# A decoder step on one core: first unit in four groups of two chunks, wide placeholder products, totals of squares tile by tile

## What is computed

```python
def rmsnorm(x, g):
    y = x * rsqrt(mean(x * x, axis=-1) + EPS)
    return y * g
def swiglu(h, w_in, w_out):
    g, u = split(h @ w_in, 2)          # w_in: 1024 x 5632
    return (silu(g) * u) @ w_out       # w_out: 2816 x 1024
for l in range(2):
    x = x + 0.5 * swiglu(rmsnorm(x, g0), w_in0, w_out0)
    ...                                # mixer
    x = x + 0.5 * swiglu(rmsnorm(x, g2), w_in1, w_out1)
y = rmsnorm(x, g_final)
```

## Time and profile before

| what | value |
|---|---|
| median of 3 runs | 1240.37 us (1240.34 to 1240.64) |
| profiled execution, whole | 1240.44 us |
| its span in the trace | 1238.6 us |
| TensorE busy in the span | 1233.2 us |
| VectorE, ScalarE, GpSimd busy | 726.1, 582.7, 81.1 us |
| DMA | 200.39 MB, mean 162 GB/s |

### The profile page before, as it was taken

How to read it: one execution, slowest core, us unless ns; L and a number is a source line. 1 busy time by engine, 2 the same in 40 slices (tenths; PEclk the granted TensorE clock), 3 DMA queues, 4 the chain that set the end, 5 groups by cost and what they waited for, 6 DMA issues and landing times.

```text
span 1238.6 us, 22056 instructions
## 1 busy us (share of the span) xinstructions
PE 1233.2 (100%) x8875; PEld 1210.4 (98%) x8875; DVE 726.1 (59%) x1127; ACT 582.7 (47%) x936; POOL 81.1 (7%) x99
## 2 busy tenths in 40 slices
PE   9999999999999999999999999999999999999998
PEld 9999999989999999999998999999998999999998
DVE  7656554575777656555564565655467585565443
ACT  6534333464556445443345554534344474544343
POOL 0000000100332000000000000000020110000010
PEclk9999999999999999999999999999999999999999
DMA  8344334543354443334543734334478734433341
GB/s 341 137 161 144 112 132 155 205 147 131 127 164 147 157 166 137 134 121 140 187 166 137 262 136 151 143 105 153 163 277 317 287 139 142 163 135 127 125 156 43
DMA packets 34778, 200.39 MB, mean 162 GB/s; under 512 B 4050, under 2 KB 4186, under 8 KB 19490
## 3 DMA queue, kind: packets, MB, share of 16 engines
q1 hardware_dynamic: 32706, 192.24, 44.0%
q0 software_dynamic: 2016, 7.39, 1.9%
HBM read 193.03 MB, written 6.57 MB: 161 GB/s over the span
## 4 chain that ended last, share of the span: by engine, by line
PE 99%; DMA 0%; SPq 0%; DVE 0%; ACT 0%; issue 0%; DVEq 0%
PE bank L556 30%; PE bank L558 30%; PE bank L557 29%; PE bank L714 1%; PE bank L713 1%; PE bank L712 1%; PE bank L716 1%; PE bank L715 1%; PE bank L1059 1%; DMA xp<-xp_in 0%; PE bank L867 0%; PE bank L822 0%; PE bank L975 0%; PE bank L1001 0%; PE bank L1007 0%; PE bank L955 0%
## 5 line engine op out<-in xcount | busy, mean ns | idle before, releaser
L556 PE MATMUL bank<-h_hi,w_hi 128*128 128x320 f32 x1792 | 555.6, 310 | 0.5 <-DVE h_lo L1682 0.5
L558 PE MATMUL bank<-h_hi,w_lo 128*128 128x320 f32 x1792 | 553.8, 309 | 0.0
L557 PE MATMUL bank<-h_lo,w_hi 128*128 128x320 f32 x1792 | 553.7, 309 | 0.0
L1222 ACT ACTIVATE w_hi<-raw 128x1024 fp32r<-128x1024 f32 (+1 forms) x364 | 331.7, 958 | 440.7 <-PE bank L558 421.7
L1668 DVE TENSOR_TENSOR w_lo<-raw,w_hi 128x1024 fp32r<-128x1024 f32 (+1 forms) x364 | 388.5, 1108 | 133.1 <-ACT w_hi L1222 133.0
L556 PEld LDWEIGHTS bank<-h_hi,w_hi 128*128 128x128 f32 x1792 | 336.3, 188 | 2.6 <-issue 1.4
L557 PEld LDWEIGHTS bank<-h_lo,w_hi 128*128 128x128 f32 x1792 | 336.4, 188 | 0.1
L558 PEld LDWEIGHTS bank<-h_hi,w_lo 128*128 128x128 f32 x1792 | 336.3, 188 | 0.0
L557 PE MATMUL bank<-f_lo,w_hi 128*128 128x320 f32 x704 | 216.5, 308 | 0.0
L558 PE MATMUL bank<-f_hi,w_lo 128*128 128x320 f32 x704 | 216.5, 308 | 0.0
L556 PE MATMUL bank<-f_hi,w_hi 128*128 128x320 f32 x704 | 216.5, 308 | 0.0
(11 more groups left out here) (263 smaller groups left out, 763.0 us busy)
## 6 DMA issues: line engine op xcount, KB each, us to landing
raw<-w_in SPq DMA_DIRECT2D x86, 1024.0 KB, 4.8
raw<-w_out SPq DMA_DIRECT2D x64, 704.0 KB, 4.0
raw<-w_a SPq DMA_DIRECT2D x12, 1024.0 KB, 4.7
raw<-w_kv SPq DMA_DIRECT2D x8, 1024.0 KB, 4.7
raw<-w_oa SPq DMA_DIRECT2D x4, 1024.0 KB, 6.0
raw<-w_q SPq DMA_DIRECT2D x4, 1024.0 KB, 4.7
raw<-w_ob SPq DMA_DIRECT2D x4, 1024.0 KB, 11.8
raw<-kc_in SPq DMA_DIRECT2D x8, 512.0 KB, 4.5
```

The costliest lines, as they stand in the source:

```text
L556: pe.matmul(out, wh, mh, start=first, stop=False)
L557: pe.matmul(out, wh, ml, start=False, stop=False)
L558: return pe.matmul(out, wl, mh, start=False, stop=last)
L1222: sc.activation(w_hi[:, n_at % 2, part * w:part * w + w], raw[:, raw_of(n_at) % RAW, part * w:part * w + w], ACT.Copy).then_inc(hi_done, 1)
```

## The change

It has three parts. `PIECES` becomes four groups of two chunks. The twelve placeholder products become four: two of 512 columns, one of 256, one of 128, all reading the same 128 columns of zeros repeatedly through a broadcast. At the end, the products of the seven chunks' sum are no longer all done ahead: each tile's come right before (tiles 1 and 2) or well before (tile 0) the products of its last chunk; the total, root and factor of tiles 1 and 2 are made for each tile alone, and TensorE's transposes are divided differently around them. ScalarE's last squares no longer wait for the seven chunks' totals.

```diff
-PIECES = ((0, 2), (2, 5), (5, 8))
+PIECES = ((0, 2), (2, 4), (4, 6), (6, 8))
+EARLY_PIECES = len(PIECES) - 2
...
-                def zeros(count):
-
-                    for _ in range(count):
-                        pe.matmul(bank[7][:, 0:128], work[:, 0:128], work[:, 128:256], start=True, stop=True)
-
-                zeros(9)
+                def zeros(blocks):
+
+                    pe.matmul(bank[7][:, 0:128 * blocks], work[:, 0:128],
+                              work[:, 128:256].unsqueeze(1).to_broadcast([128, blocks, 128]), start=True, stop=True)
+
+                zeros(4)
+                zeros(4)
                 pe.wait_ge(lo_piece, 1)
                 zeros(2)
                 pe.wait_ge(s_x[0], 16)
                 zeros(1)
...
-                    if kt == PIECES[1][0]:
-                        pe.wait_ge(lo_piece, 2)
-                    elif kt == PIECES[2][0]:
+                    if kt in (PIECES[1][0], PIECES[2][0]):
+                        pe.wait_ge(lo_piece, 2 if kt == PIECES[1][0] else 3)
+                    elif kt == PIECES[3][0]:
                         pe.wait_ge(lo_done, 1)
...
-            for t in range(3):
+            def first_squares(t):
+
                 for out, squares in token_parts(T, t):
-                    mm = pe.matmul(out, squares, ones[:, 0:1], start=(t == 0), stop=False, skip_group_check=True)
-            mm.then_inc(tok_first, 1)
+                    pe.matmul(out, squares, ones[:, 0:1], start=(t == 0), stop=False, skip_group_check=True)
...
+            first_squares(0)
             pe.wait_ge(y_gained, KT - 1)
-            turn_y(0, 0, 4)
+            turn_y(0, 0, KT - 1)
             pe.wait_ge(sq_last, 1)
             token_total(0).then_inc(tok_total, 1)
-            turn_y(0, 4, KT - 1)
             pe.wait_ge(y_gained_last, 1)
             turn_y(0, KT - 1, KT).then_inc(y_turned, 1)
+            turn_y(1, 0, 3)
             pe.wait_ge(sq_last, 2)
             pe.wait_ge(rcol_root, 1)
-            token_total(1)
+            first_squares(1)
+            token_total(1).then_inc(tok_total, 1)
+            pe.wait_ge(y_gained_last, 2)
+            turn_y(1, 3, KT).then_inc(y_turned, 1)
+            pe.wait_ge(rcol_root, 2)
+            turn_y(2, 0, 4)
+            first_squares(2)
             token_total(2).then_inc(tok_total, 1)
-            turn_y(1, 0, KT - 1)
-            pe.wait_ge(y_gained_last, 2)
-            turn_y(1, KT - 1, KT).then_inc(y_turned, 1)
-            turn_y(2, 0, KT).then_inc(y_turned, 1)
+            turn_y(2, 4, KT).then_inc(y_turned, 1)
...
-            sc.wait_ge(tok_first, 1)
...
-            token_root(2, 1, 3)
+            token_root(2, 1, 2)
             y_upper(1, 2)
-            y_upper(2, 2)
+            token_root(3, 2, 3)
+            y_upper(2, 3)
...
-            token_factor(2, 1, 3)
+            token_factor(2, 1, 2)
             y_lower(1, 2)
-            y_lower(2, 2)
+            token_factor(3, 2, 3)
+            y_lower(2, 3)
```

More of the change, by code:

```diff
@@ L193, in trunk_program @@
         hi_done = sem("weight_hi_done")
-        hi_piece = sem("first_unit_first_piece_hi_done")
+        hi_piece = sem("first_unit_early_piece_hi_done")
         lo_piece = sem("first_unit_piece_lo_done")
@@ L241, in trunk_program @@
         y_odd = sem("y_part_scaled_by_scalar")
-        tok_first = sem("first_seven_token_totals")
         mo_done = sem("last_m_gathered")
@@ L1302, in _ @@
                 sc.activation(piece(w_hi[:, 0, :], q), raw_piece(q), ACT.Copy
-                              ).then_inc(hi_done if q else hi_piece, 1)
+                              ).then_inc(hi_piece if q < EARLY_PIECES else hi_done, 1)
                 sc.wait_ge(s_x[q], 16)
@@ L1764, in _ @@
             for q, (a, e) in enumerate(PIECES):
-                if q:
-                    ve.wait_ge(hi_done, q)
+                if q < EARLY_PIECES:
+                    ve.wait_ge(hi_piece, q + 1)
                 else:
-                    ve.wait_ge(hi_piece, 1)
+                    ve.wait_ge(hi_done, q - EARLY_PIECES + 1)
                 ve.tensor_tensor(piece(w_lo[:, 0, :], q), raw_piece(q), piece(w_hi[:, 0, :], q).bitcast(f32),
```

## The result

The changed kernel takes 1245.51 us (median of 7 runs, 1242.88 to 1246.94) against 1240.37 (7 runs, 1239.96 to 1240.71). The ratio is 1.0039, 95% interval [1.0029, 1.0048]: 5.1 us slower, where 0.6 us faster was forecast, and outside the range given. The profiled execution took 1246.94, its span is 6.6 us longer than before.

What follows compares the result with a forecast made beforehand. TensorE, 99% of the chain, bounds the kernel; only idle time at its ends can go. 1240.44 - 0.45 (groups) - 0 (placeholders) - 0.1 (end) = 1239.9; the median lies 0.07 lower, so 1239.8 us, range 1239.1 to 1241.3.

Steps and rivals of the forecast that it cites:

- the first paragraph: Whole kernel: TensorE is 99% of the chain, so only its idle time at the two ends can be cut.
- part 2: Placeholders at the start: fewer, wider ones gain nothing, hidden by the wait for the first `h_lo`; at most 0.1 us lost.
- the rival of slow transfers: Start: each of two added transfers pays 2.6 us in series, unit 1 starts 4.8 late, time 1245.2; chance 0.02.
- Part 1, groups: Start, four groups: earlier transfers shorten the stall at chunk 2; 0.45 us gain kept, bounds nothing to 0.7.
- a wait of unit 1 for its `w_lo`: Start of unit 1: `w_lo` comes 0.2 to 0.25 us later, TensorE 0.6 earlier, so unit 1 starts about 14.05, not 13.9.
- the clock rival: Start: longer placeholder pause leaves 1.2 GHz until 10.6, unit 1 starts at 15.7, time 1241.5; chance 0.12.
- Part 3, the end: Totals at the end: moved products and transposes shorten TensorE's waits, 0.1 us gained; bounds 0.3 gained and 0.3 lost.
- More transfers: Start, weights and `x` in more pieces: a fixed cost per added transfer would give 1245.2 us; chance 0.02, not expected.

Runs made afterwards that it cites:

- e3: The kernel before with the four wide placeholders alone, old groups and old end kept: 1245.13 us, ratio 1.0038.
- e2: The changed kernel with 32 waiting instructions that do no work behind its two widest placeholders, restoring the instruction count: 1240.76 us, ratio 1.0002.
- e5: The kernel before with four narrow placeholders (two, one, one) in place of twelve, none wide: 1246.08 us, ratio 1.004.
- e7: The changed kernel with 16 waiting instructions behind its two widest placeholders: 1240.83 us, ratio 1.0003.
- e4: The changed kernel with 32 waiting instructions behind the attention part, just ahead of the last feed-forward part: 1245.25 us, ratio 1.0046.
- e12: The kernel before, all twelve narrow placeholders kept, with 224 waiting instructions (256 less 32) behind the first nine: 1266.5 us, ratio 1.0208.
- e6: The changed kernel with 8 waiting instructions behind its two widest placeholders: 1243.49 us, ratio 1.0023.

## Why the prediction was wrong

- **The failed step** is in the first paragraph: "The change touches just these, at the two ends of a span of 1238.6 us; the instructions between are the same." They are the same, but no longer at the same places in TensorE's stream of 256-instruction blocks. With it fails part 2, "I put this part at nothing", and its sentence "Less instruction traffic gains nothing, as TensorE waits anyway": it costs 5.1 us net, shown by e3 (the placeholders alone, +4.8) and e2 (the count restored, +0.4). I had listed no rival of this kind. That the rival of slow transfers carries the time 1245.2, near the measured 1245.5, is chance: its mechanism did not happen (below). The page of before held a hint that I passed over: 38 packets of 16 KB on the queue "instruction".
- **The Trainium skill** ("Runtime: NRT & Kernel Launch", Instruction fetch mechanics) says that instructions are refilled in blocks of 16 KiB, 256 instructions, and that crossing such a boundary is mostly hidden. The size agrees with the traces here: packets of 16384 bytes, and pauses 256 records apart. Hidden the crossings are in the kernel before, but in the changed kernel two of them cost 1.4 and 2.2 us.
- **Part 1, groups:** the direction was right, the steps only in part. x of the second group was there at 7.46 (7.0 forecast), so 0.19 of the stall at chunk 2 is left, where the prediction allowed 0.15. That gives 0.45; the first real product comes 0.08 later (6.79, 6.71 before), and 0.37 is kept. The forecast came to 0.45 another way, 0.6 less a wait of unit 1 for its `w_lo`. That wait hardly showed, because TensorE itself came later. What held the `w_lo` was not, as forecast, one more instruction on ScalarE and VectorE but the transfer: ScalarE idled 0.33 us for unit 1's first half, which landed at 4.80 + 6.9 = 11.7 (11.3 forecast). Why it landed later no run shows.
- **Part 2, the pause and the clock:** the two wide products ran 3.78 us, not 3.42, and the pause behind them was 0.51, not 0.85. Both sides of the clock rival were seen. In the changed kernel's profile the clock was up at 5.1. In e2, e3, e5 and e7 it rose at 9.8 to 10.7 (10.6 forecast) and unit 1 started at 15.3 to 15.7 (15.7 forecast). Its chance, 0.12, looks too low: that is four of the eight profiles of such kernels. It costs 1.2 us (unit 1 at 15.34 in e2, 14.14 in e4).
- **Part 3, the end:** 0.38 gained, not 0.1, and outside the bound of 0.3: the chain that counts 4.89 before counts 4.51, where the prediction looked for 4.8 to 5.0. In it the sums take 1.10 us in place of 1.31, and the transposes and last products 3.40 in place of 3.58; the pause of 0.15 for the root is part of that, the rest I can't divide. The root of the last tile didn't show, as forecast. Tile 1's store is issued 0.65 earlier, not 0.3.
- **More transfers** paid no fixed part, as forecast: unit 1's first half landed 6.9 us after its issue, 7.5 before.

Why there is a second pause, and a longer one, although its block lasts 6.9 us, stays open: behind the first pause the next fetch started 6.6 us after the block end (6.4 to 6.6 in e3, e4, e5 and e12 too, but 6.6 also in e6, which has no first pause); at the other block ends in this part it is 1.7 to 4.4 with full queues. The trace doesn't show when a block is asked for. That the 1.4 us lost at the last store come from a fetch is read from one profile and not tried; in the others the last fetch lies 1.7 to 2.0 us before TensorE's end, over 4 us after it, or in no record.

## What to carry to other kernels

Removing or adding instructions moves every block end behind them. In a long straight program, count the instructions of the engine that sets the time, and look for stretches where it uses 256 of them in a few microseconds while the DMA queues are full: here 4.3 us ahead of the first pause and 6.9 ahead of the second, against 5.7 and 6.7 without a pause before, so there is no single limit to go by. An idle of "issue" in the middle of a run of equal products, with a packet on the instruction queue that ends 1.2 to 1.6 us before work goes on, is its mark. Compare two versions of a small edit only at equal instruction counts modulo 256, or with a padding of 16 and 32 dead instructions beside them, before the edit itself is blamed or praised.

## What the runs showed of the hardware that was not expected

- A 16 KB instruction transfer took 1.0 to 1.1 us around the pauses (up to 2.4 elsewhere in these traces). With full queues it started 1.7 to 6.6 us after the block end ahead of it, and TensorE went on 1.2 to 1.6 us after its end (eleven pauses in six kernels).
- Behind the second pause (2.1 to 2.2 us of idle) the clock fell to 1.2 GHz for a stretch in the changed kernel, e3, e5, e6 and e12, and not in e4 (1.9 us): 1.4 to 2.0 us more for nearly the same idle time.
- A wait on a semaphore long passed takes TensorE's sequencer 0.106 us (e4, e12). Behind queued products 32 of them cost 1.0 us, 224 in a row 20.3.
